# Two rings for the expert rows of a PEER layer, with one gather for u and one for v, in place of one ring of joined rows

## The reference, cut to what matters

```
act = jax.nn.gelu(jnp.einsum('thkd,td->thk', expert_u[eidx], xt), approximate=False)
w = (g * act.astype(jnp.float32)).astype(expert_v.dtype)
return jnp.einsum('thk,thkd->td', w, expert_v[eidx])
```

## Time and profile before

| | |
|---|---|
| median of 3 runs | 4677.8 us (4676.13 to 4678.79) |
| the profiled execution's own time | 4673.28 us |
| its span in the trace | 4671.5 us |
| busy: TensorE, VectorE, ScalarE, GpSimd | 75%, 59%, 26%, 31% of the span |
| read from HBM, mean rate | 1294 MB, 285 GB/s |

### The profile page before, as it was taken

How to read it: one execution, slowest core, us unless ns; L and a number is a source line. 1 busy time by engine, 2 the same in 40 slices (tenths; PEclk the granted TensorE clock), 3 DMA queues, 4 the chain that set the end, 5 groups by cost and what they waited for, 6 DMA issues and landing times.

```text
span 4671.5 us, 32805 instructions
## 1 busy us (share of the span) xinstructions
PE 3487.8 (75%) x10062; PEld 1792.2 (38%) x10062; DVE 2752.9 (59%) x5414; ACT 1220.1 (26%) x2631; POOL 1447.0 (31%) x1213
## 2 busy tenths in 40 slices
PE   6799997758983788888478888865887678745564
PEld 4344443524461444445134444532444334412221
DVE  2200001367479677658976775699665655996665
ACT  1111102135211445311145552111444431110100
POOL 0111000024222344333433332344222234444553
PEclk9999997767896787798767778987676789877877
DMA  3122111469876899899888989998787789989997
GB/s 122 55 72 93 72 54 39 167 249 349 324 301 231 317 368 379 356 369 380 312 329 326 358 307 375 392 346 331 274 311 273 262 339 385 389 317 357 420 420 288
DMA packets 251084, 1331.91 MB, mean 285 GB/s; under 512 B 29880, under 2 KB 73144, under 8 KB 104448
## 3 DMA queue, kind: packets, MB, share of 16 engines
q0 software_dynamic: 163232, 1142.47, 62.5%
q1 hardware_dynamic: 87680, 187.35, 11.3%
HBM read 1294.07 MB, written 35.10 MB: 285 GB/s over the span
## 4 chain that ended last, share of the span: by engine, by line
PE 28%; DVE 27%; DMA 13%; ACT 6%; issue 6%; SPq 2%; POOL 1%; DVEq 0%; ACTq 0%; POOLq 0%
PE pv L869 12%; DVE uv L1249 11%; DMA uv<-expert_uv,rows_u 7%; PE pb L978 4%; PE pb L851 4%; PE pb L951 3%; DVE held L1273 3%; PE pb L822 2%; PE pb L926 2%; DMA arena<-w_stream 2%; DVE arena L1240 2%; SPq L700 2%; DMA arena<-out_sv_p 1%; POOL uv L776 1%; DMA uv<-expert_uv,rows_pk 1%
## 5 line engine op out<-in xcount | busy, mean ns | idle before, releaser
L776 POOL DMA_INDIRECT uv<-expert_uv,rows_u x1024 | 1311.2, 1280 | 2461.7 <-PE pv L869 1511.8
L869 PE MATMUL pv<-uv,diag 128*128 128x512 f32 x2640 | 1566.4, 753 | 598.7 <-ACT diag L1093 528.6
L1249 DVE CUSTOM_DVE_ANT_0 uv<-uv,nr 128x1024 f32<-128x1024 f32 x1056 | 1241.8, 1220 | 277.1 <-DMA uv<-expert_uv,rows_u 237.8
L869 PEld LDWEIGHTS pv<-uv,diag 128*128 128x128 f32 x2640 | 624.1, 246 | 1431.3 <-issue 1348.8
L248 PE MATMUL ps<-win,xg 128*128 128x512 f32 (+1 forms) x1440 | 631.8, 597 | 0.0
L1100 ACT ACTIVATE gel<-dots 128x4 f32<-128x4 f32 x264 | 54.2, 205 | 2049.4 <-DVE dots L1249 2049.2
L1273 DVE SCALAR_TENSOR_TENSOR held<-uv,wgt,held 128x1024 f32<-128x1024 f32 x387 | 497.3, 1285 | 13.6 <-DVE wgt L1260 0.3
L822 PE MATMUL pb<-arena 64*128 64x512 f32 (+6 forms) x544 | 265.3, 590 | 294.8 <-DMA arena<-out_sv_p 111.9
L248 PEld LDWEIGHTS ps<-win,xg 128*128 128x128 f32 (+1 forms) x1440 | 261.1, 184 | 343.9 <-issue 343.6
L851 PE MATMUL pb<-arena 128*128 128x64 f32 (+3 forms) x1728 | 320.5, 349 | 34.3 <-ACT o L1082 33.7
L851 PEld LDWEIGHTS pb<-arena 128*128 128x128 f32 (+3 forms) x1728 | 287.7, 245 | 52.9 <-issue 39.3
(11 more groups left out here) (163 smaller groups left out, 2562.8 us busy)
## 6 DMA issues: line engine op xcount, KB each, us to landing
arena<-w_stream SPq DMA_DIRECT2D x80, 1024.0 KB, 9.0
win<-w_main SPq DMA_DIRECT2D x10, 2048.0 KB, 8.8
uv<-expert_uv,rows_u POOLq DMA_INDIRECT x1024
scratch_gates<-stage POOLq DMA_DIRECT2D x32, 256.0 KB, 2.3
arena<-scratch_gates SPq DMA_DIRECT2D x8, 1024.0 KB, 22.4
xg<-x_t SPq DMA_DIRECT2D x8, 536.0 KB, 7.6
arena<-scratch_c_p SPq DMA_DIRECT2D x8, 520.0 KB, 8.0
xr<-x SPq DMA_DIRECT2D x8, 512.0 KB, 3.8
```

What stands on the lines that cost most here:

```text
L776: pool.indirect_dma_start(out=uv[k % NU][:].rearrange("p a n -> p (a n)"), out_offset=None, in_=io["expert_uv"][:, :], in_offset=bass.Indi ...
L869: mm = nc.tensor.matmul(pv[:, c * BANK:(c + 1) * BANK], diag[n % ND][:], uv[k % NU][:, 1, c * BANK:(c + 1) * BANK], start=n == first, stop ...
L1249: nc.vector.tensor_tensor_reduce(out=u, in0=u, in1=row[:], scale=1.0, scalar=0.0, op0=ALU.mult, op1=ALU.add, accum_out=dots[b % 2][:, k % ...
```

## The change

Expert u and v stay two tensors in HBM. The ring of nine joined buffers (72 KB in each partition) becomes a ring `ru` of eight u buffers and a ring `rv` of ten v buffers of 4 KB each (72 KB). GpSimd issues a gather for each. u of slot k waits for the dot of slot k - 8; v of slot k waits until v of slot k - 10 has been used, and is issued `LAG` = 3 slots after u of the same slot. The dots wait for u alone, TensorE for v, and VectorE waits for v before an accumulation. The sizes and the number of instructions on the other engines stay.

```diff
-NU = 9
+NU = 8
+NV = 10
+LAG = 3
...
-        uv = [sb(f"uv{i}", [P, 2, D]) for i in range(NU)]
+        ru = [sb(f"ru{i}", [P, D]) for i in range(NU)]
+        rv = [sb(f"rv{i}", [P, D]) for i in range(NV)]
...
-                def gather(k):
+                def gather_u(k):
                     if k >= NU:
-                        if plan.on_dve(k - NU):
-                            pool.wait_ge(summed, dve_slots[k - NU + 1])
+                        pool.wait_ge(dotted, k - NU + 1)
+                    pool.indirect_dma_start(out=ru[k % NU][:], out_offset=None, in_=io["expert_u"][:, :],
+                                            in_offset=bass.IndirectOffsetOnAxis(ap=slot_index(k), axis=0)
+                                            ).then_inc(u_in[k % NU], 16)
+
+                def gather_v(k):
+                    if k >= NV:
+                        if plan.on_dve(k - NV):
+                            pool.wait_ge(summed, dve_slots[k - NV + 1])
                         else:
-                            pool.wait_ge(valued, pe_slots[k - NU + 1])
-                    pool.indirect_dma_start(out=uv[k % NU][:].rearrange("p a n -> p (a n)"), out_offset=None,
-                                            in_=io["expert_uv"][:, :],
+                            pool.wait_ge(valued, pe_slots[k - NV + 1])
+                    pool.indirect_dma_start(out=rv[k % NV][:], out_offset=None, in_=io["expert_v"][:, :],
                                             in_offset=bass.IndirectOffsetOnAxis(ap=slot_index(k), axis=0)
-                                            ).then_inc(uv_in[k % NU], 16)
+                                            ).then_inc(v_in[k % NV], 16)
...
-                    gather(k)
+                    gather_u(k)
+                    if k >= LAG:
+                        gather_v(k - LAG)
...
+                for k in range(slots - LAG, slots):
+                    gather_v(k)
...
-                        pe.wait_ge(uv_in[k % NU], 16 * (k // NU + 1))
+                        pe.wait_ge(v_in[k % NV], 16 * (k // NV + 1))
...
-                        dve.wait_ge(uv_in[k % NU], 16 * (k // NU + 1))
-                        u = uv[k % NU][:, 0, :]
+                        dve.wait_ge(u_in[k % NU], 16 * (k // NU + 1))
+                        u = ru[k % NU][:]
...
-                        n, v = dve_slots[k], uv[k % NU][:, 1, :]
+                        n, v = dve_slots[k], rv[k % NV][:]
+                        dve.wait_ge(v_in[k % NV], 16 * (k // NV + 1))
```

More of the change, by code:

```diff
@@ L643, in stream @@
         named = sem("named")
-        uv_in = [sem(f"uv_in{i}") for i in range(NU)]
+        u_in = [sem(f"u_in{i}") for i in range(NU)]
+        v_in = [sem(f"v_in{i}") for i in range(NV)]
         dotted, gelu, weighted = sem("dotted"), sem("gelu"), sem("weighted")
@@ L869, in background @@
                             mm = nc.tensor.matmul(pv[:, c * BANK:(c + 1) * BANK], diag[n % ND][:],
-                                                  uv[k % NU][:, 1, c * BANK:(c + 1) * BANK], start=n == first, stop=n == last)
+                                                  rv[k % NV][:, c * BANK:(c + 1) * BANK], start=n == first, stop=n == last)
                         mm.then_inc(valued, 1)
@@ L1535 @@
         "sub_keys_1_t": turn(a["peer_sub_keys_1"][0]), "sub_keys_2_t": turn(a["peer_sub_keys_2"][0]),
-        "expert_uv": np.concatenate([a["expert_u"][0], a["expert_v"][0]], axis=1),
+        "expert_u": a["expert_u"][0], "expert_v": a["expert_v"][0],
     }
```

## The result

The changed kernel takes 4820.7 us (median of 4 runs, 4811.4 to 4836.6), the one before, run beside it, 4677.0. The ratio is 1.0309, 95% interval 1.0284 to 1.0334: 144 us slower, where 46 were forecast. The direction was right and the size wrong by a factor of three; the time lies 6 us above the range's end and about 100 above the forecast. The profiled execution took 4818.33 us, its span is 4816.5.

The account below looks back on a forecast made before the run. Transfers were taken to pace the tail at 2.63 us a slot, with no one resource full throughout before it. Terms 74 - 8 + 15 + 15 - 50 = +46 gave 4719, adjusted to 4724 us; range 4635 to 4815.

Parts of the forecast that it names:

- Term 1: Tail of 158 slots: two gathers pace GpSimd at 3.10 us a slot instead of 2.63; +74 us.
- The hold-off: Tail: gathers are delayed by VectorE's dots and accumulations, put at 0.63 us a slot.
- Term 2: Drain after the last gather: with GpSimd as the pace, no transfer queue stands; -8 us.
- Term 3: Three full stretches before the tail: 4 KB rows move at 385 GB/s instead of 415; +15 us, between nothing and 34.
- Term 4: Attention and merging: GpSimd's gather pairs outlast slots in two stretches, slack elsewhere; +15 us, bounds nothing and +82.
- Term 5: Before the tail: two rings give u five slots more lead, shrinking VectorE's waits; -50 us, bounds 0 and 137.
- rival B: Dense hold-off: pairs cost 3.45 us throughout, +130 in the tail, +82 before; +199, 4877 us; chance 0.13.
- Parts costed at nothing: VectorE's new wait for v, same SBUF bytes, other semaphores and TensorE's wait for v: no change in duration.
- A: Tail: the half-size gather is cheap, its time following bytes, pair 2.41 us; -36, 4642 us; chance 0.15.
- C: Before the tail: the freed waits are worth all 137 us; -41, 4637 us; chance 0.07.
- D: No change: freed waits worth 96 us cancel the rest; 4678 us; chance 0.07.
- The signs that the forecast named: Tail: gathers 0.84 to 0.94 us, no releaser, near 340 GB/s; fourth wave's u wait under 20; full stretch under 400.

Follow-up runs that it names:

- kernel 1: Kernel before, joined nine-buffer ring kept, each slot fetched by two gathers of 4 KB rows (u and v) instead of one: 4804.5 us, ratio 1.0286.
- Kernel 3: Changed kernel with v's gathers after the first ten fetching 512 bytes a row instead of 4 KB: 4682.1 us, ratio 1.0016.
- kernel 9: Kernel before with its 8 KB rows, plus one more gather a slot of 128 bytes a row into an unused buffer: 4786.6 us, ratio 1.0238.
- 15: Changed kernel with lag 0 and nine buffers each of u and v instead of eight and ten: 4806.2 us, ratio 1.0280.
- kernel 2: Changed kernel with v's gathers replaced by direct DMAs of consecutive rows, the chosen rows left out: 4636.7 us, ratio 0.9913.
- kernel 11: Kernel before's ring with two transfers a slot, u gathered, v a direct DMA of consecutive rows: 4663.9 us, ratio 0.9990.
- 14: Changed kernel with VectorE's two-input dot product replaced by a one-input sum over u: 4810.7 us, ratio 1.0299.
- The hold at the wave starts: GpSimd waits once a wave until attention's first load has landed; put into the changed kernel: 4752.3 us, ratio 1.0160.
- 10: Changed kernel with lag 0 and gathers held at each wave start until attention's first load has landed: 4727.4 us, ratio 1.0113.
- kernel 8: Old joined ring with two gathers a slot, plus gathers held at each wave start until attention's first load has landed: 4781.3 us, ratio 1.0247.
- the second trace: Changed kernel measured and traced once more, unedited: 4808.6 us, ratio 1.0303.
- Kernel 6: Kernel before with gathers held at each wave start until attention's first load has landed: 4666.8 us, ratio 0.9986.

## Why the prediction was right and wrong

**Term 1, the tail, +74: right.** 3.06 us a slot instead of the forecast 3.10, +68. The pair is GpSimd's, shown by four kernels that keep two gathers and stay at 2.98 to 3.03 whatever the bytes (1, 3, 9, 15), and by two that drop one and return to 2.62 and 2.72 (2, 11). The hold-off was put at 0.63 us a slot from chances. The gathers in the stretch 4400 to 4700 average 240.49/196 = 1.23 us, 0.29 above 0.94: 0.58 a slot, of which the dots make 0.40 (14).

**Term 2, the drain, -8: right,** -6.8.

**Term 3, 4 KB rows, +15: no sign of it.** 399 GB/s at full in kernel 2 instead of the 385 that I put from the rows: about half of the step from 415. Half of kernel 2's rows are consecutive. Where all are gathered and the engines are full, 1955 to 2175 us, the gathers' queue of the changed kernel moved 65.29 MB in 75.9% of 220 us, 391 GB/s, against 403 before in its own full stretch, 1950 to 2170: 3% less. The Trainium skill's figure ("DMA: Bandwidth & Descriptors", why small descriptors are slow) gave 1.2%, about 410; the runs lie between the two, 3 to 4% below the 8 KB rows. The term's 0.22 us a slot also compared a rate at full (385) with one at a share of 1.01 (420); like with like it is 0.20. Kernel 1, with all in 4 KB rows, lost no more before the tail than kernel 9 with 8 KB rows (65 and 74 at slot 896), and kernels 2 and 11 lost nothing (-26 and -14).

**Term 4, GpSimd during attention and merging, +15: the first step that failed.** It divided each stretch's time by its slots, found 3.04 us a pair against 3.09 a slot, and called that "fits narrowly", and elsewhere "slots come more slowly and there is slack". Slots aren't freed evenly. GpSimd idles 522.7 us for TensorE in kernel 1 and still delivers late, because after a burst it needs two gathers a slot, 2.5 us free and 2.9 to 4.6 in the burst shown, where one took 1.24 free and 1.3 to 2.3 there. Kernels 1 and 9, which double the gathers and leave the old ring alone, ran 65 and 74 us late by slot 896, with 67 and 62 us more of stalls for rows issued late; kernel 11, with the cheap second issue, was 14 early, with no more of them. So on the old ring the term was worth 65 to 75, near its bound of 82, by a mechanism that the bound (dense hold-off, rival B) didn't have. Kernel 3 sets its limit: on the two rings, with rows that land 1.4 to 2.6 us sooner, the same two gathers a slot cost nothing before the tail.

**Term 5, the freed waits, -50: the second step that failed; its waits came, its gain didn't.** VectorE waited 84 us less for u, and 1.5 us instead of 53.5 in the stretch that the term rests on (3560 to 3890, the slots that ran from 3510 to 3830 before). But the changed kernel stands at +79 to +86 at slot 896, kernel 1 at +65: the rings gave nothing instead of 50, and the medians, 4820.7 and 4808.6 against 4804.5, say the same. By the first trace that is 71 us off; with term 4's 50, and term 3's 15 the other way, it makes up the miss of 108 within 2. Crediting a wait that shrinks as time gained was the fault: two other things took it back. The hold at the wave starts brings 68 us here, about 20 on the old ring, nothing before, so the gathers that the longer u ring lets go at once cost time there. And v stands behind a waiting u: lag 0 brings 50 us. With both repaired (10) the work is only 12 us late at slot 896, 32 better than kernel 8, which has the hold on the old ring; by the medians it is 54 (4727.4 and 4781.3). So the rings can be worth about what term 5 says, and what remains of kernel 10's loss is nearly all the tail. By which waits the changed kernel loses its 79 to 86 us stays open: of its stalls for u only 23 us are of the late-issued kind, against 77 before, and its waits for v are 36 to 64 us in all before the tail, when lag 0, which removes them, brings 50.

**Parts costed at nothing.** The wait for v of VectorE before its accumulation was 11.2 us before the tail (18.4 in the second trace), small as put. That TensorE would wait for v was put at nothing: 24.5 us up to slot 896, with one of 8.8, and 45.5 in the second trace. "While the lead is eight slots v has long landed" left out that v's place in the queue is set by u's wait.

**The rivals.** A, the cheap half gather, fell: 0.93 to 0.95 us whether a row has 128 bytes (9), 512 (3), 4 KB or 8 KB. B came nearer in size (4877 and 4724 against 4821) but not in mechanism: pairs cost 3.06 in the tail, not 3.45. C and D fell. The chances had the sign (those of the rivals add up to 0.22 for faster and 0.71 for slower, where the sum says 0.21 and 0.72); the range treated terms 4 and 5 as independent small sums, when both hung on the one question of how bursts are refilled. The signs that the forecast named came true (gathers of 0.94, no waits for releases in the tail, 342 GB/s there, 1.5 us of waits for u in the last wave, 395 GB/s in a full stretch, where it was 393 before). They couldn't show the miss: those before the tail look at a wait and at a rate, and none at how slots are refilled.

**What could be gained.** Kernel 2 beats the one before but leaves out v's choice of rows. Kernel 6, the hold in the old kernel, is not told apart from it (0.9971 to 1.0002). No complete kernel here beats the one before.

## What to carry to other kernels

A gather has a fixed price on the engine that issues it, so splitting one into two doubles that price whatever the bytes; compare it with the pace of the slots, and with the time between frees within a burst, not with the mean over a stretch. An idle sum on the issuing engine is no slack if the consumer waits right after each burst. To tell late issue from slow transfer, take for each stall the time from the end of the gather's issue to the start of the instruction that waited. With two rings fed from one in-order queue, each ring waits for the other's slot, and gathers released early run beside somebody's load: try the lag at zero, and look at the first load of each stage, before counting the waits that a deeper ring frees.

## What the hardware showed unexpectedly

- An indirect DMA of 128 rows takes GpSimd 0.93 to 0.95 us free, and 0.30 before the next, for rows of 128 bytes to 8 KB; a direct one of 128 rows of 4 KB takes 0.56 (median of 1056 in kernel 2).
- A gather beside a two-input VectorE instruction of 1.2 us ends about 0.9 us after it; beside a one-input sum of the same length it isn't held (0.94). A direct DMA isn't held beside two-input ones either: the 73 that started during one after 4400 us in kernels 2 and 11 took 0.54 to 0.57.
- At full, 4 KB rows, half of them consecutive, moved 399 GB/s and 8 KB rows 415; beside attention's loads gathers moved 391 with 4 KB rows and 403 with 8 KB.
